# Segment 0 of the gated recurrence placed inside the last six groups of the projection, its loads reordered, GpSimd's first key copies tied to the last masks

## The chip, the cores and the metric

The kernel runs on one core of one Trainium2 chip, in one launch. The metric is the time of one execution on the device, in microseconds (us), as the median of several runs. A core has five engines that work side by side, each through its own instruction stream: TensorE (PE in the profile; PEld is its weight load), VectorE (DVE), ScalarE (ACT), GpSimd (POOL) and SyncE (SP, which here only issues DMAs). They order each other by semaphores. SBUF is the memory that the engines work on, PSUM the banks into which TensorE writes.

## The reference: what is computed

One layer of a hybrid decoder: an input projection, two token mixers on its result, gates, an output projection and a layer norm. There are 2048 prompt tokens and 64 sample tokens. Mixer A is a dilated sliding-window attention. The part around the change is mixer B, a gated linear recurrence with 4 heads and a state of 128 x 128 per head:

```
h = x @ w_in                      # split into qa, ka, va, ga, qb, fb, ib, gb
f = lb + (1 - lb) * sigmoid(fb);  k = 1 - f;  v = ib;  q = silu(qb) * 128 ** -0.5
S_t = diag(f_t) S_{t-1} + k_t v_t^T;   o_t = S_t^T q_t        # per head
a_out = attention(qa, ka, va) * silu(ga);  b_out = rmsnorm(o) * silu(gb)
y = layernorm(2 ** 0.25 * x + concat(a_out, b_out) @ w_out)
```

## The kernel before

The program is written by hand as one instruction stream for each engine, in five stages: a projection with the features on partitions (`project_transposed`: q, k and the forget gate), a second projection with the tokens on partitions (`project_natural`: v, i and the two gates), the prompt's recurrence (`hgrn_prompt`), the prompt's attention and the output projection (`attend_and_project`). The streams of the last four are concatenated, engine by engine, in `build`: each engine ends one stage and goes into the next by itself, held only by semaphores.

**The second projection** is 68 groups (`NGR`), numbered `n`. A group is 8 k steps of 3 matmuls (the exact product of split fp32 values: high x high, high x low, low x high), L757, with 512 columns each, into one of two PSUM banks. Two groups make one tile `j` of 128 tokens; the last tile, groups 66 and 67, has the 64 sample tokens. VectorE splits the x of a tile (`split_x`, L487 and L489), ScalarE evacuates each group (`evacuate`, L668), SyncE stores it to `projN` (L381). Between the groups, by a schedule in `n`, the samples' recurrence and attention are done; the last of these steps, the values of the eighth sample batch (L824), is behind group 60 (`LAST + 4`). Once SyncE has loaded the masks and q and the sigmoid of the gate for segments 0 and 1 (behind group 57, `load_segment`, L870 and L871), ScalarE makes the keys `kd` and forget factors `fd` of segment 0 beside groups 61 to 64, one head each (L740, L742).

**The recurrence** cuts the prompt into 4 segments of 512 tokens (`NSEG`, index `s`), and each into 4 chunks of 128. A segment has 18 scores (`NA`, index `j`): 4 of diagonal blocks (`ND`, L1121) and 14 for 7 levels of halves, two head pairs each (L1131). A diagonal score is 4 matmuls in fp32, a level's 8; the profile shows each such matmul as two. A level's score reads `qd` and `kd`; VectorE then widens both by the forget factors (`widen`: three tensor_tensor, L1058, L1059, L1061), which the score two places later waits for, and copies the score out of PSUM under a mask (`keep`: L1071 for diagonal blocks, L1080 for levels). Three PSUM banks hold scores. Before the first level VectorE forms `qd` by `first_products` (L1051). The state work of a segment stands between the scores of the next: `turn_keys` (L1143) behind scores 0 to 3, then, by the tuples `DELTA` and `OUT`, `delta` (L1154) and `read_out` (L1165, L1166) behind scores 4 to 11 in turns. ScalarE copies the turned keys (L1008) and the outputs (L1013), and takes their squares (L995); VectorE updates the state (`advance`, L1089). So segment 0 has only scores on TensorE, as nothing precedes it. Its diagonal scores start behind group 67, and TensorE takes 18 of them in a row.

**Loads and buffers.** Buffers of the recurrence come in pairs, `s % 2`. SyncE's `load(s)` waits until segment `s - 2` is done with q and gates, loads them and the values `v` (L948, from `projN`). In the loop, `load(s + 1)` stands behind `store(s - 1)`, which waits for ScalarE's copy of the last output of that segment. ScalarE's `decays(s)` (L984, L987) makes keys and forget factors of segment 1 ahead of all outputs and of segment 2 and 3 behind the outputs of segments 0 and 1. The buffers lie where the projection's were, so that what overlies its x, weights or stage waits for `group_done` or `stage_free`.

**GpSimd** clears `at0` behind the last samples and `at1` behind the last group, loads the first pair of heads' keys and queries (L878), and sorts them by dilation: `sort(0, 1)` and `sort(0, 2)`, three copies of 128 x 2048 each (L1420). The first waits for segment 3's fourth score (`a_done`), the second stands behind a pair load that waits for the squares of segment 3. Attention (scores L1783, minima L1529, exponentials L1686, turns L1797, values L1811) needs the first sorted keys at its ninth unit; its first three units are scored between the last read-outs.

## Time and profile before

| | before |
|---|---|
| median of 3 runs | 1592.74 us (1588.07 to 1593.78) |
| the profiled execution, its time | 1590.03 us |
| its span, first to last instruction | 1588.2 us |
| TensorE busy | 1530.3 us (96%) |
| VectorE busy | 774.5 us (49%) |
| ScalarE busy | 502.5 us (32%) |
| GpSimd busy | 442.4 us (28%) |
| mean granted TensorE clock | 0.966 |

Times in the profile are microseconds from the start of the span. The granted clock is a share of TensorE's full 2.4 GHz; the shares between come from stretches at 2.4 and at 1.2 GHz. A matmul's duration overlaps the next one's, so the cost of a matmul is read from start to start.

### The profile page before, as it was taken

Reading aid. Unit: us, or ns where it says so; the run is one execution under the profiler, and the core shown is the slowest. Engines: PE = TensorE matmul, PEld = TensorE weight load, DVE = VectorE, ACT = ScalarE, POOL = GpSimd, SP = SyncE. Lnnn points to the kernel's source line nnn. Section 1 sums busy time; section 2 is a strip of 40 time slices with the busy share of each in tenths; the row PEclk is TensorE's granted clock in tenths of the full one; section 3 lists DMA queues with packets and bytes.
Section 4 is the critical chain, followed back from the end, with each engine's and each line's share of the span. In section 5 each row is a group of like instructions: output and inputs, shape, how many; then the busy total and the mean of one; then the engine's idle time right before and its main releaser. Section 6 shows DMA issues by size and latency. Waiting matters only on the chain.

```text
span 1588.2 us, 25524 instructions
## 1 busy us (share of the span) xinstructions
PE 1530.3 (96%) x9802; PEld 1374.1 (87%) x9802; DVE 774.5 (49%) x1941; ACT 502.5 (32%) x1426; POOL 442.4 (28%) x281
## 2 busy tenths in 40 slices
PE   7999999998999999899999999889999999999997
PEld 7999999996788777677788999789999999888885
DVE  6022010004323214121215799867677777798884
ACT  5111111113110114122322032228677777432231
POOL 1233210000420000000001000306987779344442
PEclk9999999998999999999998699799999999999998
DMA  9999996234695867866665558749896981976641
GB/s 309 339 329 352 340 322 187 81 111 131 205 296 178 316 213 256 305 213 212 200 204 129 125 186 234 215 150 241 170 207 149 203 184 63 292 240 199 220 159 53
DMA packets 174501, 338.34 MB, mean 213 GB/s; under 512 B 15635, under 2 KB 115283, under 8 KB 165523
## 3 DMA queue, kind: packets, MB, share of 16 engines
q1 hardware_dynamic: 141452, 169.18, 35.1%
q10 hardware_dynamic: 22432, 111.29, 21.9%
q0 software_dynamic: 10512, 56.48, 13.1%
q8 instruction: 65, 1.06, 0.3%
q14 instruction: 40, 0.33, 0.1%
HBM read 262.25 MB, written 155.39 MB: 263 GB/s over the span
## 4 chain that ended last, share of the span: by engine, by line
PE 66%; DMA 4%; DVE 4%; ACT 1%; issue 1%; SPq 0%; DVEq 0%; ACTq 0%
PE banks L757 21%; PE banks L1846 11%; PE banks L1811 7%; PE banks L1131 7%; PE banks L1783 6%; PE banks L1797 4%; DMA spare<-in_xT 2%; DMA partials<-a_stage 2%; PE banks L824 1%; PE banks L1121 1%; PE banks L806 1%; PE banks L1154 1%; PE banks L1165 1%; PE banks L1166 1%; PE banks L1827 1%
## 5 line engine op out<-in xcount | busy, mean ns | idle before, releaser
L256 PE MATMUL acc<-xhi,whi 128*128 128x424 f32 (+1 forms) x640 | 227.3, 355 | 8.2 <-DVE xlo L235 8.2
L757 PE MATMUL banks<-nwhi,nxhi 128*128 128x512 f32 (+1 forms) x544 | 219.3, 403 | 11.8 <-DVE nwlo L494 6.6
L256 PE MATMUL acc<-xlo,whi 128*128 128x424 f32 (+1 forms) x640 | 227.0, 355 | 0.0
L256 PE MATMUL acc<-xhi,wlo 128*128 128x424 f32 (+1 forms) x640 | 226.9, 355 | 0.0
L1420 POOL CAST a_sorted<-a_plain 128x2048 fp32r<-128x2048 f32 x45 | 172.2, 3882 | 178.7 <-PE banks L1121 144.6
L757 PE MATMUL banks<-nwlo,nxhi 128*128 128x512 f32 (+1 forms) x544 | 214.4, 394 | 0.0
L757 PE MATMUL banks<-nwhi,nxlo 128*128 128x512 f32 (+1 forms) x544 | 214.1, 394 | 0.0
L1686 ACT ACTIVATE a_prob<-a_prob,a_stage 128x256 f32<-128x256 f32 (+1 forms) x384 | 174.1, 454 | 76.1 <-DVE a_stage L1529 73.7
L1529 DVE CUSTOM_DVE_ANT_0 a_prob<-banks,a_bias 128x256 f32<-128x256 f32 (+1 forms) x384 | 125.3, 364 | 77.6 <-PE banks L1783 69.1
L1811 PE MATMUL banks<-a_v,a_probT 128*128 128x64 f32 x1200 | 157.6, 269 | 2.9 <-DVE a_probT L1541 2.8
L1811 PEld LDWEIGHTS banks<-a_v,a_probT 128*128 128x128 f32 x1200 | 150.1, 193 | 4.3 <-DVE a_probT L1541 3.4
L487 DVE CAST nxhi<-spare 128x1024 fp32r<-128x1024 f32 (+1 forms) x34 | 24.9, 732 | 251.2 <-DMA spare<-in_xT 175.8
L225 DVE CAST whi<-wraw 128x1024 fp32r<-128x1024 f32 x16 | 14.9, 932 | 258.8 <-PE acc L256 166.5
L668 ACT ACTIVATE nstage<-banks 128x512 f32<-128x512 f32 (+1 forms) x68 | 40.6, 597 | 312.8 <-PE banks L757 312.6
L757 PEld LDWEIGHTS banks<-nwhi,nxhi 128*128 128x128 f32 (+1 forms) x544 | 101.5, 187 | 41.4 <-DVE nxlo L489 11.6
L275 ACT ACTIVATE stage<-acc 128x424 f32<-128x424 f32 (+1 forms) x80 | 41.7, 524 | 296.4 <-PE acc L256 295.9
L1131 PE MATMUL banks<-qd,kf 128*128 128x64 f32 x896 | 126.8, 307 | 8.4 <-DVE kf L1061 7.9
L1131 PEld LDWEIGHTS banks<-qd,kf 128*128 128x128 f32 x896 | 124.5, 225 | 9.9 <-issue 9.8
L256 PEld LDWEIGHTS acc<-xhi,whi 128*128 128x128 f32 x640 | 121.1, 189 | 10.6 <-issue 8.5
L256 PEld LDWEIGHTS acc<-xhi,wlo 128*128 128x128 f32 x640 | 121.1, 189 | 2.1
L256 PEld LDWEIGHTS acc<-xlo,whi 128*128 128x128 f32 x640 | 121.1, 189 | 2.1
L757 PEld LDWEIGHTS banks<-nwhi,nxlo 128*128 128x128 f32 (+1 forms) x544 | 101.4, 186 | 24.6 <-issue 1.4
(214 smaller groups left out, 2552.4 us busy)
## 6 DMA issues: line engine op xcount, KB each, us to landing
a_plain<-split_qk POOLq DMA_DIRECT2D x48, 512.0 KB, 12.9
out_kwin_s<-in_cache_kT ACTq DMA_DIRECT2D x8, 2048.0 KB, 19.9
split_qk<-spare POOLq DMA_DIRECT2D x16, 1024.0 KB, 14.5
spare<-in_xT SPq DMA_DIRECT2D x32, 512.0 KB, 7.1
projN<-nstage SPq DMA_DIRECT2D x32, 512.0 KB, 6.2
qg<-in_cache_kT ACTq DMA_DIRECT2D x8, 2048.0 KB, 11.3
kf<-in_cache_v ACTq DMA_DIRECT2D x8, 2048.0 KB
out_kwin_s<-in_cache_kT ACTq DMA_DIRECT2D x8, 2032.0 KB, 29.6
```

The costliest lines, as they stand in the source:

```text
L256: mm = pe.matmul(acc[:, j, 0:n], w[:, u, k], x[:, k, c0:c0 + n], start=(k == 0 and a == 0), stop=(k == KD - 1 and a == 2))
L275: nc.scalar.activation(stage[:, u, c0:c0 + n], acc[:, j, 0:n], func).then_inc(bank_free, 1)
L668: nc.scalar.activation(stage[0:m, u, g * H:(g + 1) * H], acc[0:m, n % 2], ACT.Copy if j < NTL else ACT.Silu).then_inc(evacuated, 1)
L757: mm = pe.matmul(acc[0:m, n % 2], x[:, u, k, 0:m], w[:, k, g * H:(g + 1) * H], start=(k == 0 and b == 0), stop=(k == KD - 1 and b == 2))
L1131: mm = pe.matmul(a_ps[:, i % 3, a * CH // 2:(a + 1) * CH // 2].rearrange("p (n j) -> p n j", j=w), kd[u][:, h, t0:t0 + CH], late, start=Tr ...
L1420: nc.gpsimd.tensor_copy(dst[:, n].rearrange("p (r m) -> p r m", r=d), src[:, n].bitcast(F32).rearrange("p (m r) -> p r m", r=d)).then_inc( ...
L1529: ins = nc.vector.tensor_tensor_reduce(prob[:, n % 4, w, 2 * P - m:], s_ps[:, n % 3, w * 2 * P + 2 * P - m:(w + 1) * 2 * P], bias[g % 2][: ...
L1686: ins = nc.scalar.activation(pr, pr, ACT.Exp, bias=to[:, DA + 1:DA + 2], scale=-1.0, accum_out=to[:, DA:DA + 1])
L1783: mm = pe.matmul(s_ps[:, n % 3, w * 2 * P + (2 - m) * P:(w + 1) * 2 * P], source[:, 0, q0:q0 + P], source[:, 1 + a, k0:k0 + m * P], start= ...
L1797: mm = pe.transpose(t_ps[:, n % 3, a * P:(a + 1) * P], prob[:, n % 4, w, place * P:(place + 1) * P], ident[:])
L1811: mm = pe.matmul(o_ps[:, (n // 4) % 2, col:col + DA], probT[:, n % 3, a], v[g % 2][:, c, vt, x * DA:(x + 1) * DA], start=(a == 0 or ts[a - ...
L1846: mm = pe.matmul(z_ps[w][0:n, g], m[:, w, k, 0:n], ww[:, g * H:(g + 1) * H], start=(k == 0 and a == 0), stop=(k == KD - 1 and a == 2))
```

## The change

- TensorE issues the 18 scores of segment 0 inside groups 62 to 67, ahead of the k steps numbered in `SLOTS` (k step 0 is the first of group 62): diagonal blocks ahead of steps 6, 7, 8 and 9, levels ahead of 11, 13, 16, 18, 21, 24, 26, 29, 31, 34, 37, 39, 42 and 44. The function `score` is moved out of `tensor` for this and otherwise unchanged. The recurrence's own stream starts with segment 1.
- ScalarE makes the keys of segment 0 behind group 60's evacuation and its forget factors behind group 61's; those of segment 1, one head each, behind groups 63 to 66.
- VectorE's last x split (tile 33) goes behind the ninth score of segment 0. The first memset of the state moves from segment 0 to segment 1.
- `kf1`, `qd1`, `at0` and `qd0` now lie where no buffer lives that groups 62 to 67 use.
- SyncE loads v of segment 0 behind the last group, then q and gates of segment 2 at once; in the loop, q and gates of segment `s + 2` are loaded behind the values of `s + 1`.
- `DELTA` and `OUT` go back by two scores.
- GpSimd's `sort(0, 1)` waits for all masks of segment 3.

```diff
@@ -330,7 +330,7 @@
             sem(f"d_{n}") for n in ("v_landed", "const", "bias_landed", "zeroed", "q_done", "qk_done", "min_done", "nm_done"))
         e_done, r_done, t_done, pt_done, pv_done, o_done = (
             sem(f"d_{n}") for n in ("e_done", "r_done", "t_done", "pt_done", "pv_done", "o_done"))
-        first["samples_done"], first["bias_spread"] = o_done, b_repeated
+        first["samples_done"], first["bias_spread"], first["out_free"] = o_done, b_repeated, out_free
...
+            first["last_split"] = lambda: split_x(NTL * NPASS - 1)
...
-                if n % 2 and j + 2 < NTL * NPASS:
+                if n % 2 and j + 2 < NTL * NPASS - 1:
                     split_x(j + 2)
...
@@ -731,16 +732,15 @@
                 if n == 2 * NTL - 1:
                     for k in range(KD):
                         round_w(3, k)
-                if LAST + EACH <= n < LAST + EACH + HB:
-                    h, (kd0, fd0) = n - LAST - EACH, (first["kf"][:, 0], first["kf"][:, 1])
-                    if h == 0:
-                        act.wait_ge(first["qk_landed"][0], 32)
-                        act.wait_ge(pv_done, NB)
-                    lb, oml, noml = (lbs_[:, m, h:h + 1] for m in (1, 2, 3))
-                    nc.scalar.activation(kd0[:, h], first["sg"][:, 0, h], ACT.Identity, bias=oml, scale=noml
-                                         ).then_inc(first["kd_done"], 1)
-                    nc.scalar.activation(fd0[:, h], first["sg"][:, 0, h], ACT.Identity, bias=lb, scale=oml
-                                         ).then_inc(first["fk_done"], 1)
+                if n == LAST + EACH - 1:
+                    act.wait_ge(pv_done, NB)
+                    first["keys"](act, 0, range(HB))
+                if n == LAST + EACH:
+                    first["forgets"](act, 0, range(HB))
+                if NGR - 5 <= n < NGR - 1:
+                    h = n - NGR + 5
+                    first["keys"](act, 1, range(h, h + 1))
+                    first["forgets"](act, 1, range(h, h + 1))
...
+                    if n >= NGR - 6:
+                        first["early_scores"](pe, KD * (n - NGR + 6) + k)
...
+        kf1, qd1, at0, qd0 = sb("kf1", [P, 2, HB, SEG]), wide("qd1"), attn("at0"), wide("qd0")
+        khn0, ost0, v31, ost1 = (rows(n) for n in ("khn0", "ost0", "v31", "ost1"))
+        v30, at1, khn1 = rows("v30"), attn("at1"), rows("khn1")
+        S = sb("S", [P, 2, HB, DB])
+        qd, at, khn, v, ost = (qd0, qd1), (at0, at1), (khn0, khn1), (v30, v31), (ost0, ost1)
+        kd, fd = ([first["kf"][:, m], kf1[:, m]] for m in range(2))
...
-        TURN, DELTA, OUT = (0, 1, 2, 3), (4, 6, 8, 10), (5, 7, 9, 11)
+        TURN, DELTA, OUT = (0, 1, 2, 3), (6, 8, 10, 12), (7, 9, 11, 13)
+        SLOTS = [6 + j for j in range(ND)] + [11 + 13 * j // 5 for j in range(NA - ND)]
...
-            def load(s):
+            def load_rows(s):
                 u, t0 = s % 2, s * SEG
                 if s >= 2:
-                    sp.wait_ge(fk_done, HB * (s - 1))
-                    sp.wait_ge(q1_done, NG2 * (s - 1))
-                    sp.wait_ge(a_done, NA * (s - 2) + ND)
-                    load_segment(sp, projT, s, q, sg, qk_landed)
-                    for m in range(2):
-                        sp.wait_ge(first["stage_free"][m], 16 * (T // P + 1))
                     sp.wait_ge(o_done, NCK * (s - 1))
                 sp.dma_start(v[u][:], projN[t0:t0 + SEG, WB:2 * WB].rearrange("(c p) v -> p c v", p=P)
                              ).then_inc(v_landed[u], 16)
+
+            def reload_segment(s):
+                sp.wait_ge(fk_done, HB * (s - 1))
+                sp.wait_ge(q1_done, NG2 * (s - 1))
+                sp.wait_ge(a_done, NA * (s - 2) + ND)
+                load_segment(sp, projT, s, q, sg, qk_landed)
 
...
-            load(0)
             sp.wait_ge(first["group_done"], NGR)
+            load_rows(0)
+            reload_segment(2)
             for u in range(2):
                 sp.wait_ge(first["stage_free"][u], 16 * (T // P + 1))
-            load(1)
+            load_rows(1)
...
-                    load(s + 1)
+                    load_rows(s + 1)
+                if s >= 1 and s + 2 < NSEG:
+                    reload_segment(s + 2)
...
+        def keys(act, s, heads):
+            u = s % 2
+            act.wait_ge(qk_landed[u], 32 * (s // 2 + 1))
+            for h in heads:
+                nc.scalar.activation(kd[u][:, h], sg[:, u, h], ACT.Identity, bias=oml[:, h:h + 1], scale=noml[:, h:h + 1]
+                                     ).then_inc(kd_done, 1)
+
+        def forgets(act, s, heads):
+            u = s % 2
+            for h in heads:
+                nc.scalar.activation(fd[u][:, h], sg[:, u, h], ACT.Identity, bias=lb[:, h:h + 1], scale=oml[:, h:h + 1]
+                                     ).then_inc(fk_done, 1)
+
+        first["keys"], first["forgets"] = keys, forgets
+
         def scalar(act):
             def decays(s):
                 u = s % 2
-                act.wait_ge(qk_landed[u], 32 * (s // 2 + 1))
-                if s >= 2:
-                    act.wait_ge(s_done, NCK * (s - 1) + 1)
-                    act.wait_ge(t_done, NCK * (s - 1))
-                for h in range(HB):
-                    ins = nc.scalar.activation(kd[u][:, h], sg[:, u, h], ACT.Identity, bias=oml[:, h:h + 1], scale=noml[:, h:h + 1])
-                ins.then_inc(kd_done, HB)
-                for h in range(HB):
-                    ins = nc.scalar.activation(fd[u][:, h], sg[:, u, h], ACT.Identity, bias=lb[:, h:h + 1], scale=oml[:, h:h + 1])
-                ins.then_inc(fk_done, HB)
+                act.wait_ge(s_done, NCK * (s - 1) + 1)
+                act.wait_ge(t_done, NCK * (s - 1))
+                keys(act, s, range(HB))
+                forgets(act, s, range(HB))
 
...
+                if s == 1:
+                    for x in range(2):
+                        act.wait_ge(first["stage_free"][x], 16 * (T // P + 1))
...
-            decays(1)
-            for u in range(2):
-                act.wait_ge(first["stage_free"][u], 16 * (T // P + 1))
...
                 first_products(s)
-                if s == 0:
+                if s == 1:
                     dve.wait_ge(first["group_done"], NGR)
                     nc.vector.memset(S[:, 0], 0.0).then_inc(s_done, 1)
...
+                    if s == 0 and j == 2 * ND:
+                        first["last_split"]()
...
+        def early_scores(pe, slot):
+            if slot == SLOTS[0]:
+                pe.wait_ge(const, 16 * 3)
+                pe.wait_ge(qk_landed[0], 32)
+                pe.wait_ge(kd_done, HB)
+            if slot in SLOTS:
+                score(pe, 0, SLOTS.index(slot))
+
+        first["early_scores"] = early_scores
...
-            pe.wait_ge(const, 16 * 3)
-            for s in range(NSEG):
+            for s in range(1, NSEG):
                 pe.wait_ge(qk_landed[s % 2], 32 * (s // 2 + 1))
                 pe.wait_ge(kd_done, HB * (s + 1))
                 for j in range(NA):
-                    score(s, j)
-                    if s >= 1:
-                        if j in TURN:
-                            turn_keys(s - 1, TURN.index(j))
-                        if j in DELTA:
-                            delta(s - 1, DELTA.index(j))
-                        if j in OUT:
-                            read_out(s - 1, OUT.index(j))
+                    score(pe, s, j)
+                    if j in TURN:
+                        turn_keys(s - 1, TURN.index(j))
+                    if j in DELTA:
+                        delta(s - 1, DELTA.index(j))
+                    if j in OUT:
+                        read_out(s - 1, OUT.index(j))
...
+            sp.wait_ge(keep["ms_done"], NCK * (NSEG - 1))
...
-            pool.wait_ge(keep["a_done"], 18 * (NSEG - 1) + 4)
-            pool.wait_ge(keep["q1_done"], HB // 2 * NSEG)
+            pool.wait_ge(keep["mask_done"], 18 * NSEG)
             sort(0, 1)
```

## Rows read from the trace of the kernel before

**Rows 1.** Page, the chain that ended last, share of the span by engine
```profile
PE 66%; DMA 4%; DVE 4%; ACT 1%; issue 1%; SPq 0%; DVEq 0%; ACTq 0%
```

**Rows 2.** Busy time by stretch: us, busy (count) of each engine, clock, DMA share, GB/s
```profile
862.90:900.40 37.50, 37.49 (x176) 37.50 (x177) 26.44 (x45) 0.00 (x0) 0.00 (x0) 0.50 0.85 200
932.60:944.20 11.60, 11.41 (x98) 10.98 (x96) 11.24 (x24) 1.93 (x10) 0.00 (x0) 1.00 0.87 298
1014.90:1026.80 11.90, 11.88 (x57) 11.90 (x58) 11.79 (x21) 0.00 (x0) 0.00 (x0) 0.51 0.56 172
```

**Rows 3.** Timeline of TensorE, segment 0: start, us, engine, line, what, [idle before]
```profile
852.19 3.73 PE L1121 MATMUL banks<-qg,kf 128*128 128x128 f32 x32
862.91 37.78 PE L1131 MATMUL banks<-qd,kf 128*128 128x64 f32 x176 [1.08 <-DVE kf L1061]
900.49 1.81 PE L1121 MATMUL banks<-qg,kf 128*128 128x128 f32 x7
```

**Rows 4.** Timeline of VectorE, from segment 1 to the start of segment 2
```profile
909.51 0.69 DVE L1058 TENSOR_TENSOR qd<-qd,kf 128x512 f32<-128x512 f32 x1 [1.23 <-PE banks L1131]
946.11 0.72 DVE L1080 COPY_PREDICATED at<-lmask,banks 128x512 f32<-128x512 int32 x1
949.99 2.36 DVE L1051 TENSOR_TENSOR qd<-qg,kf 128x1024 f32<-128x1024 f32 x2 [3.16 <-issue]
956.41 0.69 DVE L1058 TENSOR_TENSOR qd<-qd,kf 128x512 f32<-128x512 f32 x1 [0.55 <-PE banks L1131]
```

**Rows 5.** Timeline of ScalarE, the keys of segment 2
```profile
944.15 0.81 ACT L984 ACTIVATE kf<-qg,bounds 128x512 f32<-128x512 f32 x1 [9.45 <-DMA qg<-projT]
```

**Rows 6.** Timeline of VectorE, segment 3
```profile
1004.07 2.23 DVE L1058 TENSOR_TENSOR qd<-qd,kf 128x512 f32<-128x512 f32 x1 [1.50 <-PE banks L1131]
1010.60 4.17 DVE L1061 TENSOR_TENSOR kf<-kf 128x512 f32<-128x512 f32 x1
1052.81 0.73 DVE L1080 COPY_PREDICATED at<-lmask,banks 128x512 f32<-128x512 int32 x1
```

**Rows 7.** Timeline of GpSimd, the first and the second set of copies
```profile
1001.85 12.37 POOL L1420 CAST a_sorted<-a_plain 128x2048 fp32r<-128x2048 f32 x3 [144.57 <-PE banks L1121]
1084.82 11.24 POOL L1420 CAST a_sorted<-a_plain 128x2048 fp32r<-128x2048 f32 x3
```

**Rows 8.** Timeline of TensorE, scores, a turn and a read-out at full clock
```profile
904.76 1.06 PE L1121 MATMUL banks<-qg,kf 128*128 128x128 f32 x8
905.70 0.63 PE L1143 MATMUL banks<-ident,kf 128*128 128x128 f32 x4
910.25 1.90 PE L1131 MATMUL banks<-qd,kf 128*128 128x64 f32 x16
911.99 0.44 PE L1165 MATMUL banks<-S,qd 128*128 128x128 f32 x2
```

**Rows 9.** Timeline of TensorE, projection matmuls directly after the samples' attention values
```profile
779.82 0.50 PE L757 MATMUL banks<-nwhi,nxhi 128*128 128x512 f32 x1
780.16 0.39 PE L757 MATMUL banks<-nwlo,nxhi 128*128 128x512 f32 x1
780.39 0.40 PE L757 MATMUL banks<-nwhi,nxlo 128*128 128x512 f32 x1
```

**Rows 10.** Timeline of SyncE's queue, the loads of v for segments 0 and 1
```profile
853.69 2.85 SPq L948 DMA_DIRECT2D v<-projN  x2
```

**Rows 11.** Tile v, time to landing: the load for segment 0, then for segment 1
```profile
DMA to landing us min/median/max: 9.8/9.8/9.8
DMA to landing us min/median/max: 24.2/24.2/24.2
```

**Rows 12.** Timeline of TensorE, the first scores that read sorted keys
```profile
1082.76 0.71 PE L1783 MATMUL banks<-a_sorted 128*128 128x128 f32 x4
```

**Rows 13.** VectorE by line and shape, 1085 to 1096 us, then 1073 to 1084 us
```profile
L1529 DVE CUSTOM_DVE_ANT_0 a_prob<-banks,a_bias 128x256 f32<-128x256 f32 x11 | 4.3, 421 | 1.5 <-PE banks L1783 1.5
L1529 DVE CUSTOM_DVE_ANT_0 a_prob<-banks,a_bias 128x256 f32<-128x256 f32 x11 | 4.3, 422 | 6.8 <-PE banks L1783 6.8
```

55 lines of the change are left out of this document (28 added, 27 removed).

## The prediction, made before the changed kernel was run

> **What bounds the kernel now.** I read the chain of waits of the page first: TensorE makes 66% of it, no other engine more than 4% [rows 1]. So an edit pays by the time that it takes out of TensorE's own sequence, and other engines' work counts where TensorE waits for it or runs slowly. The busy shares hide the second kind, so I listed the granted clock by stretch around the change. From 862.9 to 900.4 us TensorE is shown 100% busy at 0.50 of its clock, that is 1.2 of 2.4 GHz, and from 1014.9 to 1026.8 at 0.51; in between, from 932.6, it is 1.00 [rows 2]. Then I read the timelines of each engine there. They show four places that the change touches. (a) Segment 0 of the recurrence: only scores, from 852.19 to 900.49 us, with no state work to put between them; TensorE and VectorE hand each other work, and after a gap of 1.08 us the clock is at half [rows 3]. (b) Segments 1 to 3: from its first widening at 909.51 to its last mask's end at 946.83 VectorE hardly rests, so there it sets the pace and not TensorE. (c) The starts of segments 2 and 3: VectorE idles over 3 us [rows 4], as TensorE does, behind ScalarE's keys, and ScalarE waited 9.45 us for the loads [rows 5], which SyncE issued behind the store of the segment before. (d) Segment 3: GpSimd's three copies run from 1001.85 to 1014.2 us [rows 7], and three tensor_tensor of VectorE in a row, otherwise 0.69 us each, are stretched: the first takes 2.23, the last 4.17 us [rows 4, 6]. TensorE has to wait for them and then runs at half clock [rows 2].
>
> **Step A, segment 0 between the groups.** The 48.30 us from 852.19 to 900.49 leave the sequence [rows 3]. The same 18 scores come back inside groups 62 to 67. At full clock a score of diagonal blocks takes 0.94 us (904.76 to 905.70) and one of a level 1.74 us (910.25 to 911.99) [rows 8], so 4 x 0.94 + 14 x 1.74 = 28.1 us. No row shows a switch in the middle of an accumulation; the nearest is the samples' attention between groups: the first matmul behind it is followed after 0.34 us, the next after the usual 0.23 us [rows 9]. I take 0.1 us into a score and 0.1 out of it, 18 x 0.2 = 3.6 us, with 0 and 0.5 us as ends (0 to 9 us); below 0 is excluded, as the scores' matmuls and loads remain what they are. Is the pace kept? A k step is three matmuls or 0.68 us and the slots of the levels lie two or three steps apart, so such a score comes every 2 x 0.68 + 1.74 + 0.2 = 3.3 us or more. VectorE takes 37.3 us in segment 1 for 14 levels and four updates, under 2.7 us a level [rows 4]. So no stall. The six groups are 144 matmuls of 0.227 us, 32.7 us, so group 62 starts at 819.5 and the first score is due six k steps later, at 823.6. Its keys, four activations of 0.8 us [rows 5], move up from groups 61 to 64 into group 60; the forget factors follow group 61, done by 823, VectorE's products (2.4 us, as in segment 1) by 826.5, and the first level's score comes at 831. The last x split (1.1 us) now stands behind the ninth score, some 10 us before group 66 needs it. ScalarE's eight activations of segment 1 (6 us, formerly behind the groups) go between evacuations over 5 us apart: hidden. Net of A: 48.3 - 28.1 - 3.6 = 16.6 us gained.
>
> **Step A2, the start of segment 1.** Now 9.02 us pass from its first score to the first widening (900.49 to 909.51) [rows 3, 4], the first part at half clock. Coming from the groups the clock is full: four scores with a turn each, the turn half as many rows as the score, are 4 x (0.94 + 0.47), and the fifth score is 1.74 [rows 8], together 7.4 us. VectorE is ready earlier: its last mask of segment 0 ends about when the groups do; then 2.4 us of products, 0.5 of memset, 3.3 of masks. Gain 1.6 us. GpSimd's memset, still tied to the last group, is done before the first mask. New on this path: segment 0's values are wanted by the first delta, now behind the seventh score, 7.4 + 1.74 + 1.74 + 0.4 of waiting = 11.3 us after the last group. They can only be loaded when the groups are done. Now they are issued 1.5 us after that [rows 10] and land in 9.8 us, together 11.3 [rows 11]: no stall to speak of. The other load of this size took 24.2 us, which is the bad end (14.4 us).
>
> **Step B, loads ahead of stores.** Segment 2's q and gates are asked for directly after the last group and segment 3's one segment early, so ScalarE finds them. Its keys must still follow the squares of the last read-out, which moves two scores back, to some 27.4 us after the first widening; with 2 us of copy and squares the keys are done at 32.4 and the forget factors at 35.3 us, where TensorE's last score ends at 34 and VectorE's last mask at 37.3 us. Both are in time, the second by 2 us. What is late next is VectorE: 2.4 us of products, 3.2 of masks, and about 0.9 us of waiting for the fifth score, 6.5 us. A segment then lasts 37.3 + 6.5 = 43.8 us from widening to widening, where it is 46.9 (909.51 to 956.41) and 47.7 us (956.41 to 1004.07) [rows 4, 6]. Gain 3.1 + 3.9 = 7.0 us. The shift of DELTA and OUT changes no amount of VectorE's work: nothing.
>
> **Step C, GpSimd's copies.** Segment 3 lasts 49.5 us from its first widening to its last mask's end (1004.07 to 1053.54) [rows 6], against 37.3 us in segment 1. The copies move behind the last mask: 12.2 us gained. They take 12.4 us there and are first read at 1082.76 us, 29 us after that mask [rows 12]. The second set starts at 1084.82 [rows 7] behind a pair load that waits for the squares of segment 3: unchanged. Under the copies now lie four state updates of VectorE and the first attention minima, whose first input is in PSUM. Such minima take a mean of 421 ns beside the second set of copies and 422 before it [rows 13], so they aren't held; no row shows a state update beside a copy. I take nothing, as for the minima, and 8 us as the other end (two updates held 3.5 us each, as the last tensor_tensor is, and a little clock); below nothing is excluded, since nothing runs faster for the copies. The Trainium skill, "SBUF — State Buffer", section "Who interferes with whom", says that a VectorE instruction with two SBUF inputs contends with a GpSimd one that reads SBUF and one with a single SBUF input doesn't. The stretched tensor_tensor and the minima agree with it; by it the updates cost nothing, by the bound 8 us.
>
> **Sum.** 16.6 + 1.6 + 7.0 + 12.2 = 37.4 us. The profiled execution took 1590.03 us (span 1588.2), so 1590.0 - 37.4 = 1552.6; it lies 2.7 us under the median of the three runs, 1592.74, so 1555.3, given as 1555. Attention behind it only shifts.
>
> **Rivals.**
> 1. The copies hold the tail. The updates stand between TensorE's last read-outs, so they would be on the path: 8 us, 1563. For it: the stretched instructions [rows 6]. Against: those read SBUF twice, and the minima aren't stretched [rows 13]. 12%.
> 2. Segment 0's values land late, as the second such load did: 14.4 us, 1570. For it: GpSimd's pair load and SyncE's other loads run in the same 30 us, and 2 MB are added [rows 11]. Against: the values are first in their queue. 8%.
> 3. The loads are there, but segments 2 and 3 start no earlier, because ScalarE's keys, now behind a later read-out, become the wait: none of the 7.0 us, 1562. The margin of 2 us speaks against it. 7%.
> 4. Slower than before: the clock falls to half inside the groups. The place is the work from group 62 to 67 (32.7 + 28.1 + 3.6 = 64.4); each us of that work at half clock costs one us more, so it would have to last over 37 us of that work to eat the gain, and over the whole stretch it would give 1555 + 64.4 = 1619. For it: the same scores ran 37.5 us at 0.50 with TensorE fully busy and did not get the clock back by themselves [rows 2, 3]. Against: from 932.6 to 944.2, a stretch of nearly nothing but such scores, it kept 1.00 [rows 2], and here each is followed by six or more projection matmuls, and there is no gap. 4%. The Trainium skill, "TensorE: Matmul & The Clock Gate", "What's actually happening", has sustained activity release the throttle; by that rule the clock would soon come back and this rival be void. The trace doesn't bear it out: the stretch at 0.50 is fully busy.
>
> **How the numbers follow.** Forecast 1555 with 66% (own range 1549 to 1562: switches 0 to 9 us, spread of the runs), the rivals 12, 8, 7 and 4%, the rest 3% for what I don't see. The low end is the forecast less the 3.6 us of switches and 3.4 of spread, 1548. The high end takes in rivals 1 to 3, 1572. About 0.5% (8 us) is what a measurement of this kernel can tell from no change. Faster 94%, same 2%, slower 4%.
>
> **What would show it.** A: the six groups with 18 scores last 64 to 65 us at a clock near 1.0, and segment 1's first score follows the last group directly; VectorE's masks of segment 0 lie among the groups. A2: no wait for v at the first delta. B: no DMA wait ahead of the keys of segments 2 and 3, widening to widening 43.8 us. C: no VectorE tensor_tensor above 1 us in segment 3, 37.3 us from widening to mask; the four updates at 1.1 us each. Wrong it would be if a switch costs over 1 us, if a segment stays at 47 us, or if a new gap of TensorE shows up in the first 15 us of segment 1 or of attention.

## The result and the profile after

The changed kernel takes 1558.26 us in the median (1554.11 to 1562.63, 4 runs); the kernel before, run on the same chip, 1593.26 us (1588.07 to 1596.22, 4 runs). The ratio is 0.9784 (95% interval 0.9769 to 0.9798), so 35.0 us faster, where 1555 us and a gain of 37.4 were predicted.

| | after |
|---|---|
| median of 4 runs | 1558.26 us |
| the profiled execution, its time | 1562.63 us |
| its span | 1560.8 us |
| TensorE busy | 1506.6 us (97%) |
| VectorE, ScalarE, GpSimd busy | 768.2, 502.0, 440.1 us |
| mean granted TensorE clock | 0.984 |

The page of after, its chain that ended last, share of the span by engine: TensorE still sets the time [rows 1].

```profile
PE 63%; DVE 4%; DMA 4%; ACT 2%; issue 1%; POOL 1%; SPq 0%; DVEq 0%; ACTq 0%; POOLq 0%
```

This execution was the longest of the four. Its group 62 starts at 823.43 us, 4.0 us later than in the trace of before (819.39), although the code ahead of it is the same, and it loses some 4 us more far behind the change, in attention. So I compare from the start of group 62 to the first score on sorted keys: 263.4 us before (819.39 to 1082.76), 227.3 after (823.43 to 1050.69), 36.1 us less. Fifteen us on, 1.0 of these is given back (below). The 35.1 us left agree with the medians. By the steps of the prediction:

| stretch | before | after | gain | predicted |
|---|---|---|---|---|
| A: groups 62 to 67 and the 18 scores of segment 0 | 81.1 | 61.45 | 19.65 | 16.6 |
| A2: first score of segment 1 to first widening | 9.02 | 7.48 | 1.5 | 1.6 |
| B: first widening of segment 1 to that of segment 3 | 94.6 | 92.0 | 2.5 | 7.0 |
| C: first widening of segment 3 to its last mask | 49.5 | 38.5 | 11.0 | 12.2 |
| last mask to first sorted score | 29.2 | 27.8 | 1.4 | 0 |

Timeline of TensorE in after: the first score inside group 62, with the k step behind it, and a level's score inside group 67; then segment 1's first score and its turn; last, the start of segment 3.

```profile
827.51 1.05 PE L1144 MATMUL banks<-qg,kf 128*128 128x128 f32 x8
828.32 0.48 PE L759 MATMUL banks<-nwhi,nxhi 128*128 128x512 f32 x1
828.64 0.40 PE L759 MATMUL banks<-nwlo,nxhi 128*128 128x512 f32 x1
...
829.11 1.05 PE L1144 MATMUL banks<-qg,kf 128*128 128x128 f32 x8
...
880.39 1.89 PE L1154 MATMUL banks<-qd,kf 128*128 128x64 f32 x16
882.09 0.42 PE L759 MATMUL banks<-nwhi,nxhi 128*64 128x512 f32 x1
...
884.88 1.05 PE L1144 MATMUL banks<-qg,kf 128*128 128x128 f32 x8
885.77 0.60 PE L1177 MATMUL banks<-ident,kf 128*128 128x128 f32 x4
...
975.14 1.44 PE L1144 MATMUL banks<-qg,kf 128*128 128x128 f32 x8 [2.06 <-issue]
```

Read the starts: a diagonal score holds the sequence for 0.81 us (827.51 to 828.32), a level's for 1.70 (880.39 to 882.09), and the k step behind a diagonal score takes 0.79 us instead of 0.68 (828.32 to 829.11), as its second matmul starts 0.32 us after its first and not 0.23. Nothing idles. Segment 3, however, starts after a gap of 2.06 us.

Busy time by stretch in after, columns as in [rows 2]: groups 62 to 67, segment 1, 25 us across the start of segment 2, segment 3, and the 15 us ahead of the first sorted score.

```profile
823.50:884.90 61.40, 61.40 (x402) 53.01 (x401) 42.84 (x67) 12.02 (x18) 0.00 (x0) 1.00 0.13 40
892.40:930.90 38.50, 36.38 (x318) 35.63 (x318) 36.90 (x73) 13.15 (x44) 0.00 (x0) 1.00 1.12 289
916.20:941.20 25.00, 23.42 (x203) 22.66 (x202) 22.42 (x41) 10.25 (x24) 0.00 (x0) 1.00 1.00 307
984.40:1022.90 38.50, 35.46 (x310) 34.77 (x310) 36.85 (x72) 7.51 (x36) 0.00 (x0) 1.00 0.67 195
1035.80:1050.60 14.80, 11.72 (x92) 11.53 (x91) 9.34 (x41) 13.11 (x60) 0.00 (x0) 0.88 0.62 198
```

Both stretches at half clock in [rows 2] have gone. The DMA engines, nearly idle beside the groups (0.13), are saturated in segment 1 and beyond.

VectorE in after: the first wait inside segment 1, the products and the first widening of segment 3, and the first of the four last updates.

```profile
922.62 0.69 DVE L1080 TENSOR_TENSOR qd<-qd,kf 128x512 f32<-128x512 f32 x1 [1.00 <-PE banks L1154]
977.95 2.36 DVE L1073 TENSOR_TENSOR qd<-qg,kf 128x1024 f32<-128x1024 f32 x2 [2.30 <-issue]
984.38 0.69 DVE L1080 TENSOR_TENSOR qd<-qd,kf 128x512 f32<-128x512 f32 x1 [0.90 <-PE banks L1154]
1026.45 1.12 DVE L1111 SCALAR_TENSOR_TENSOR S<-S,kf,banks 128x128 f32<-128x128 f32 x4 [3.60 <-PE banks L1188]
```

Three of these updates (1026.45, 1029.57 and 1032.70 us) lie beside GpSimd's copies, which end at 1034.5; the fourth (1035.85) and the first minima (from 1036.89) come behind them. No stretched tensor_tensor is left, where [rows 6] has 2.23 and 4.17 us. GpSimd in after, both sets of copies, and TensorE's first score on the second set:

```profile
1022.91 11.62 POOL L1453 CAST a_sorted<-a_plain 128x2048 fp32r<-128x2048 f32 x3 [132.94 <-DVE at L1102]
1054.06 11.21 POOL L1453 CAST a_sorted<-a_plain 128x2048 fp32r<-128x2048 f32 x3
```
```profile
1065.32 0.66 PE L1815 MATMUL banks<-a_sorted 128*128 128x128 f32 x4 [0.43 <-POOL a_sorted L1453]
```

The second set is now a wait: TensorE idles 0.43 us for it. From the first sorted score to this one TensorE takes 14.63 us, where it took 13.63 before, so from there on the lead over the kernel before is 1.0 us smaller: 0.6 us of that stands at this score, the other 0.4 ahead of the second sorted score.

Last, ScalarE and SyncE's queue in after. ScalarE had finished the squares at 967.6 us and then waited 4.51 us for segment 3's gates, where [rows 5] has 9.45; the second row is the first of four copies of the samples' cache, 2 MB each, that ScalarE issues beside segment 2's keys.

```profile
972.11 0.81 ACT L990 ACTIVATE kf<-qg,bounds 128x512 f32<-128x512 f32 x1 [4.51 <-DMA qg<-projT]
```
```profile
922.23 0.57 ACTq L130 DMA_DIRECT2D out_vwin_s<-in_cache_v  x1
```

SyncE's queue (start, how long the issue held the queue, line, what):

```profile
889.41 19.11 SPq L971 DMA_DIRECT2D a_ident<-in_ident  x1
...
916.16 25.00 SPq L896 DMA_DIRECT2D a_v<-projN  x4
941.21 10.29 SPq L898 DMA_DIRECT2D a_v<-projN  x1
951.55 6.30 SPq L961 DMA_DIRECT2D o_b<-ost  x1
957.89 0.91 SPq L949 DMA_DIRECT2D v<-projN  x1
958.91 2.22 SPq L872 DMA_DIRECT2D qg<-projT  x1
```

The loads that attention needs much later (`a_ident`, `a_v`) hold the queue from 889 to 951 us, and the store of segment 0 to 958. Segment 3's gates are asked for at 958.91, though everything they wait for in the code was long done.

### The profile page after: what moved, and what is told of

Same layout as the page of the kernel before. It is cut to its first block, busy times and chain, and to the rows that moved or that the text cites. A ratio compares the mean times of both kernels' runs of the same rounds, so it can differ in the third digit from the quotient of the medians.

```text
span 1560.8 us, 25524 instructions
## 1 busy us (share of the span) xinstructions
PE 1506.6 (97%) x9802; PEld 1348.0 (86%) x9802; DVE 768.2 (49%) x1941; ACT 502.0 (32%) x1426; POOL 440.1 (28%) x281
## 4 chain that ended last, share of the span: by engine, by line
PE 63%; DVE 4%; DMA 4%; ACT 2%; issue 1%; POOL 1%; SPq 0%; DVEq 0%; ACTq 0%; POOLq 0%
PE banks L759 22%; PE banks L1878 11%; PE banks L1843 7%; PE banks L1815 5%; PE banks L1154 4%; PE banks L1829 4%; DMA spare<-in_xT 2%; PE banks L826 1%; DMA partials<-a_stage 1%; DVE at L1102 1%; PE banks L808 1%; PE banks L1859 1%; PE banks L1144 1%; DVE kf L1081 1%; PE banks L1199 1%
## 5 line engine op out<-in xcount | busy, mean ns | idle before, releaser
L759 PE MATMUL banks<-nwhi,nxhi 128*128 128x512 f32 (+1 forms) x544 | 220.6, 405 | 13.3 <-DVE nwlo L494 6.9
L256 PEld LDWEIGHTS acc<-xhi,whi 128*128 128x128 f32 x640 | 121.4, 190 | 11.7 <-issue 7.9
L759 PEld LDWEIGHTS banks<-nwlo,nxhi 128*128 128x128 f32 (+1 forms) x544 | 101.8, 187 | 21.4 <-issue 1.2
L1154 PEld LDWEIGHTS banks<-qd,kf 128*128 128x128 f32 x896 | 105.0, 192 | 6.4 <-issue 4.8
## 6 DMA issues: line engine op xcount, KB each, us to landing
qg<-in_cache_kT ACTq DMA_DIRECT2D x8, 2048.0 KB, 11.6
```

The lines of the kernel that those rows point to most:

```text
L256: mm = pe.matmul(acc[:, j, 0:n], w[:, u, k], x[:, k, c0:c0 + n], start=(k == 0 and a == 0), stop=(k == KD - 1 and a == 2))
L759: mm = pe.matmul(acc[0:m, n % 2], x[:, u, k, 0:m], w[:, k, g * H:(g + 1) * H], start=(k == 0 and b == 0), stop=(k == KD - 1 and b == 2))
L1154: mm = pe.matmul(a_ps[:, i % 3, a * CH // 2:(a + 1) * CH // 2].rearrange("p (n j) -> p n j", j=w), kd[u][:, h, t0:t0 + CH], late, start=Tr ...
```

## The experiments

Each time is a median, set against runs of the kernel before on the same chip (their medians lie between 1592.6 and 1593.4 us). Segment lengths are from the first widening to the end of the last mask, read from the trace of each kernel. Of the versions of the changed kernel, only e3_old_loads and e9_sort_twice have an interval clear of its own (ratio 0.9769 to 0.9798). For the others the traces decide. In the order of the sections below the versions are e1_copies_late, e2_copies_in_seg3, e9_sort_twice, e3_old_loads, e10_loads_first, e7_attention_loads_later, e5_old_turns, e6_old_turns_2_3 and e8_both, and e4_fill_seg0; I call them e1 to e10 for short.

### GpSimd's copies alone

```diff
-            pool.wait_ge(keep["a_done"], 18 * (NSEG - 1) + 4)
-            pool.wait_ge(keep["q1_done"], HB // 2 * NSEG)
+            pool.wait_ge(keep["mask_done"], 18 * NSEG)
```

> The kernel before with one edit: GpSimd's first three sort copies wait for all masks of segment 3. Theory (the copies hold VectorE's tensor_tensor, and only those): segment 3 from first widening to last mask goes from 49.5 to 37.3 us, the tail stays, total 11 to 12 us less. Rival (the copies hold the state updates too): 3 to 8 us less, with updates over 1.1 us in the tail.

1581.78 us, ratio 0.9913 (0.9879 to 0.9947), so 11.6 us faster. Segment 3 takes 37.31 us (1003.79 to 1041.10) instead of 49.47, the three updates beside the copies 1.12 us each, as the fourth behind them. Step C is worth what the working said, 12.2 us in the trace.

### Extra copies in segment 3 of the changed kernel

```diff
+            pool.wait_ge(keep["a_done"], 18 * (NSEG - 1) + 4)
+            pool.wait_ge(keep["q1_done"], HB // 2 * NSEG)
+            pool.wait_ge(pair_landed[0], 96)
+            for n in range(3):
+                nc.gpsimd.tensor_copy(plain[0][:, n], plain[0][:, n].bitcast(F32)).then_inc(keep["extra"], 1)
+            pool.wait_ge(keep["extra"], 3)
             pool.wait_ge(keep["mask_done"], 18 * NSEG)
```

> The changed kernel plus three extra GpSimd copies of the same size (in place, same values) at the place where the kernel before had them, behind the fourth score of segment 3; all else as in the changed kernel. Theory: 11 to 12 us more, three tensor_tensor of 2 to 4.3 us and a TensorE gap of 6 us with half clock behind it. Rival (copies beside segment 3 are harmless once the other waits are gone): under 3 us more.

1562.69 us, ratio 0.9803 (0.9778 to 0.9828), 4.4 us over the changed kernel. The expectation missed, for a reason that the trace gives: these copies, in place and without a stride, took 6.03 us together and not 12. GpSimd, then VectorE in segment 3:

```profile
977.14 6.03 POOL L1502 CAST a_plain<-a_plain 128x2048 fp32r<-128x2048 f32 x3 [89.80 <-PE banks L1144]
```
```profile
979.28 2.13 DVE L1080 TENSOR_TENSOR qd<-qd,kf 128x512 f32<-128x512 f32 x1 [0.89 <-PE banks L1154]
981.34 2.37 DVE L1081 TENSOR_TENSOR kf<-kf 128x512 f32<-128x512 f32 x1
983.74 0.69 DVE L1083 TENSOR_TENSOR kf<-kf 128x512 f32<-128x512 f32 x1
```

Two tensor_tensor are held and the third, behind the last copy, is not. Segment 3 takes 46.15 us (38.47 without), 7.7 more; in this run its loads were in time, which gave some 2.4 back. The size was left in doubt, so I ran the real copies twice.

### The strided copies made twice

The same edit, with the three copies of `sort(0, 1)` in the place of the plain ones:

```diff
+                nc.gpsimd.tensor_copy(sorted_[0][:, n].rearrange("p (r m) -> p r m", r=DILS[1]),
+                                      plain[0][:, n].bitcast(F32).rearrange("p (m r) -> p r m", r=DILS[1])).then_inc(keep["extra"], 1)
```

> The changed kernel, with the same three strided copies of GpSimd also made once more where they stood before, at segment 3's fourth score (the set behind the last mask stays as it is). Theory (a tensor_tensor of VectorE is held to the end of the copy that it meets, so the price follows the copies' length): the set takes 11 to 12 us as at its old place, where three unstrided copies took 6.0 us and cost segment 3 7.7 us; segment 3 goes from 38.5 to 48.5 to 50 us from widening to last mask, and the time is 1558 + 11 = 1569 us. Rival (the price is a fixed stall at the start of a set, whatever the length): segment 3 again 46 us and 1563 to 1566 us.

1564.97 us, ratio 0.9833 (0.9815 to 0.9851), 6.7 us over the changed kernel. GpSimd and VectorE:

```profile
977.23 12.29 POOL L1502 CAST a_sorted<-a_plain 128x2048 fp32r<-128x2048 f32 x3 [90.23 <-PE banks L1144]
```
```profile
979.37 2.28 DVE L1080 TENSOR_TENSOR qd<-qd,kf 128x512 f32<-128x512 f32 x1 [0.89 <-PE banks L1154]
981.58 4.29 DVE L1081 TENSOR_TENSOR kf<-kf 128x512 f32<-128x512 f32 x1
985.90 4.18 DVE L1083 TENSOR_TENSOR kf<-kf 128x512 f32<-128x512 f32 x1
```

Segment 3 takes 49.37 us, as before the change (49.47): 10.9 us for 12.3 of copies, 7.7 for 6.0. The rival, a price that doesn't depend on the length, is out. But the price is not in proportion to the length either. VectorE's three instructions are stretched by 3.1 us in the run before this one and by 8.7 us here, and that part follows the copies. The rest, 4.6 and 2.2 us, lies behind: TensorE idled 3.55 and 9.10 us for VectorE and then ran at a clock of 0.50 until about 996 us in both traces. The time, 1565, lies under the 1569 expected; segment 3 starts 2.0 us earlier in this run than in the trace of after, since its loads were in time, and the rest is within the intervals.

### The loads behind the store again

```diff
             load_rows(0)
-            reload_segment(2)
...
                 if s >= 1 and s + 1 < NSEG:
+                    reload_segment(s + 1)
                     load_rows(s + 1)
-                if s >= 1 and s + 2 < NSEG:
-                    reload_segment(s + 2)
```

> The changed kernel with the q and gate loads of segments 2 and 3 back behind the store of the segment before. Theory: the starts of segments 2 and 3 wait for loads again, widening to widening 47 to 49 us for segment 1 (44.8 in the changed kernel) and about 48 for segment 2 (47.2, as segment 3's load is late there anyway), total 3 to 5 us more. Rival (VectorE bounds, loads hidden): within 1 us.

1571.52 us, ratio 0.9861 (0.9835 to 0.9886), 13.3 us over the changed kernel: far more than either theory gave. TensorE at the starts of segments 2 and 3:

```profile
934.70 2.05 PE L1142 MATMUL banks<-qg,kf 128*128 128x128 f32 x8 [10.29 <-issue]
972.54 7.59 PE L1152 MATMUL banks<-qd,kf 128*128 128x64 f32 x64
987.24 2.05 PE L1142 MATMUL banks<-qg,kf 128*128 128x128 f32 x8 [7.11 <-issue]
```

The gaps were about 3 us in the kernel before, whose scores behind the last read-out of segment 1 are these:

```profile
932.59 11.69 PE L1131 MATMUL banks<-qd,kf 128*128 128x64 f32 x96
```

Two things add up, and I had named neither. First, this kernel keeps the shift of `DELTA` and `OUT`. The store, and the loads behind it, wait for the last read-out, and behind that lie 7.6 us of scores (972.54 to 980.1) where there were 11.7. That is 4.1 us more of waiting, which alone gives the gap ahead of segment 3: its loads take as long as before (11.5 us from the copy of the last output to the keys, 11.4 before). Second, at segment 2 that path takes 14.7 us: its gates go out at 919.64 us, beside the attention loads, and ScalarE waits 12.75 us for them. So the early loads are a condition of the shift, and not only a gain of 7 us beside it. What the old loads cost without the shift was not run.

### The early loads alone, in the kernel before

```diff
             sp.wait_ge(first["group_done"], NGR)
+            reload_segment(2)
...
                     load(s + 1)
+                if s >= 1 and s + 2 < NSEG:
+                    reload_segment(s + 2)
```

Here `load(s)` no longer loads q and gates.

> The kernel before with step B alone: q and gates of segment 2 are asked for behind the last group, those of segment 3 in the loop one segment early, behind the values of segment 2. Theory of the prediction: both starts are 6.5 us long, the segments 43.8 us, gain 7.0 us, 1586 us. Rival, from the changed kernel's trace: segment 3's loads stand in SyncE's queue behind the loads for attention and land late, so only segment 2 gains: 3 us, 1590 us.

1584.51 us, ratio 0.9949 (0.9932 to 0.9965), 8.1 us faster. The first widenings stand at 911.03, 954.70 and 998.36 us, so 43.67 and 43.66 us from one to the next; the working said 43.8. Taken alone, step B was right. In SyncE's queue the last attention load went out at 891.95 us, with all of segment 1 still ahead, and segment 3's gates at 935.97:

```profile
882.42 9.48 SPq L894 DMA_DIRECT2D a_v<-projN  x4
891.95 0.83 SPq L896 DMA_DIRECT2D a_v<-projN  x1
935.41 0.44 SPq L944 DMA_DIRECT2D v<-projN  x1
935.97 1.05 SPq L870 DMA_DIRECT2D qg<-projT  x1
```

### The attention loads behind segment 3's

In the changed kernel, `load_bias` and `load_values(0)` move into SyncE's loop, to its third pass, behind segment 3's q, gates and values:

```diff
             sp.wait_ge(first["bias_spread"], 32)
-            load_bias(sp, rep_p, keep["bias"][0], 0, keep["bias_landed"][0])
-            load_values(sp, projN, keep["v"][0], 0, keep["v_landed"][0])
...
+                if s == 2:
+                    load_bias(sp, rep_p, keep["bias"][0], 0, keep["bias_landed"][0])
+                    load_values(sp, projN, keep["v"][0], 0, keep["v_landed"][0])
```

> The changed kernel with SyncE's bias and value loads for attention moved from ahead of the segment loop to behind the loads of segment 3. Theory (the late start of segment 3 comes from these loads holding SyncE's queue, so that the store of segment 0 and the loads behind it are issued some 25 us late): segment 3's loads are issued before 935 us, ScalarE does not wait for them, TensorE's gap of 2 us ahead of segment 3 is gone, widening to widening 44.8 us in place of 47.2, total 2 us less. Rival (the values for attention then land late): a new wait at the first values matmul of attention, total 3 us or more above the changed kernel.

1555.48 us (1552.86 to 1556.64), ratio 0.9762 (0.9749 to 0.9775), 2.8 us under the changed kernel. SyncE's queue and ScalarE's keys of segment 3:

```profile
917.82 0.37 SPq L961 DMA_DIRECT2D o_b<-ost  x1
...
918.84 1.05 SPq L872 DMA_DIRECT2D qg<-projT  x1
```
```profile
963.75 0.81 ACT L991 ACTIVATE kf<-qg,bounds 128x512 f32<-128x512 f32 x1
```

The wait of 4.51 us and TensorE's gap of 2.06 us are gone, segment 3's start is 6.3 us long as segment 2's, and `a_v`, asked for at 966 us, is still in time. The time agrees; its interval overlaps that of the changed kernel, so the verdict rests on the trace.

How much the late loads cost differs from one execution to the next. e2_copies_in_seg3 and e9_sort_twice have the same code for SyncE as the changed kernel, and it takes 44.8 and 45.2 us in them from segment 2's first widening to segment 3's, against 47.2 in the trace of after. ScalarE waits 1.02 and 2.54 us for the gates. ScalarE's first cache copy and SyncE's queue in e2_copies_in_seg3:

```profile
919.59 0.57 ACTq L130 DMA_DIRECT2D out_vwin_s<-in_cache_v  x1
```
```profile
911.07 9.62 SPq L896 DMA_DIRECT2D a_v<-projN  x4
...
921.53 30.19 SPq L961 DMA_DIRECT2D o_b<-ost  x1
...
952.99 1.21 SPq L872 DMA_DIRECT2D qg<-projT  x1
```

Here the attention loads are out by 921.5 us, and it is the store of segment 0 that is held for 30 us. In all five traces that have the attention loads ahead of the loop and the early loads (after, e2, e5, e6, e9) the cache copies are issued at 918 to 922 us, and segment 3's gates only at 952 to 959, whatever stood in the queue meanwhile. In this kernel the store, the values and the gates of segment 3 go out from 917.8 to 921.1 us, around the cache copies at 918.5, and each took 1.2 us or less; the four `a_v` loads that follow the next cache copies (963.3) were held 37.6 us. So what the attention loads do is to push these loads behind the cache copies. A kernel with the cache copies moved would test it and was not run.

### The state work at its old places

```diff
-        TURN, DELTA, OUT = (0, 1, 2, 3), (6, 8, 10, 12), (7, 9, 11, 13)
+        TURN, DELTA, OUT = (0, 1, 2, 3), (4, 6, 8, 10), (5, 7, 9, 11)
```

> The changed kernel with the state work back behind scores 4 to 11 in all segments. The changed kernel's VectorE waits 1.0 us for a score in each of segments 1 to 3 and takes 38.5 us from first widening to last mask, where the kernel before took 37.3. Theory (the two-score shift costs that): 37.3 us again in segments 2 and 3, but in segment 1 the first delta now comes 3.5 us ahead of the landing of segment 0's values, so nothing is won there; total 2 us less. Rival (the shift is neutral and the 1.2 us come from elsewhere): segments stay at 38.5 us, total 1 to 3 us more through the wait for the values.

1560.12 us, ratio 0.9797 (0.9781 to 0.9813), 1.9 us over the changed kernel; 2 under it was expected. Segments 2 and 3 did get shorter, 37.35 and 37.33 us instead of 38.48. But segment 1 takes 42.57. TensorE there:

```profile
890.93 1.60 PE L1188 MATMUL banks<-v,khn 128*128 128x128 f32 x8 [1.79 <-DMA v<-projN]
892.33 3.51 PE L1154 MATMUL banks<-qd,kf 128*128 128x64 f32 x16
```

The first delta now comes before segment 0's values: a wait of 1.79 us, and behind it a score takes 3.51 us instead of 1.90. From 892 to 899 us the granted clock was 0.55. So the shift pays in segment 1, 4.1 us (42.57 for 38.49), and costs 1.1 us in each of the others. Step A2 had used this without saying so: its first delta stands "behind the seventh score", which is the shift's doing. From the first widening of segment 2 to that of segment 3 this kernel takes 43.67 us, Step B's 43.8.

### The shift in segment 1 only, without and with the later attention loads

```diff
+                    back = 0 if s == 1 else 2
-                    if j in DELTA:
-                        delta(s - 1, DELTA.index(j))
+                    if j + back in DELTA:
+                        delta(s - 1, DELTA.index(j + back))
```

and the same for `read_out` and for VectorE's `advance`.

> The changed kernel with the state work back behind scores 4 to 11 in segments 2 and 3 only; segment 1 keeps the shift. Theory: 37.3 us in segments 2 and 3, 38.5 in segment 1, no wait for values, total 2 to 3 us less than the changed kernel. Rival: no change within 1 us.

1556.18 us (1555.32 to 1559.2), ratio 0.9773 (0.9759 to 0.9787), 2.1 us under the changed kernel, as expected. The segments take 38.49, 37.33 and 37.33 us. The start of segment 3 is still late (9.8 us), as ScalarE waits 9.22 us for its gates.

> Both edits of the two runs before in one kernel. Theory: segments 1 to 3 at 38.5, 37.3 and 37.3 us, both boundaries at 6.4 us, total 4 to 5 us less than the changed kernel, about 1553 where that one is 1558. Rival: the two do not add up, 1556 or more.

1553.91 us (1552.22 to 1559.42), ratio 0.9761 (0.9744 to 0.9779), 4.4 us under the changed kernel and 39 under the one before: the fastest version. Its segments take 38.49, 37.36 and 37.34 us and both starts 6.3. From each other the three variants are not separated by their times, only by these lengths.

### Filling TensorE in segment 0 of the kernel before

```diff
                 for j in range(NA):
                     score(s, j)
+                    if s == 0 and j >= ND:
+                        pe.matmul(s_ps[:, 0], ident[:], q[:, 0, 0], start=True, stop=True)
```

> The kernel before with one extra fp32 matmul of 512 columns, whose result nobody reads, behind each of the 14 level scores of segment 0, some 0.9 us each at full clock. Theory (segment 0's slowness is mostly the clock, which falls because the scores alone do not keep it up): the clock stays at or returns to 1.0, segment 0 takes about 42 us in place of 48.3, total 6 us less although work is added. Rival (the clock stays at half): 14 x 1.7 = 24 us more. Third (the wait between TensorE and VectorE is what counts, clock or not): no change within 2 us.

1582.78 us, ratio 0.9929 (0.9904 to 0.9954): 10.6 us faster with 14 matmuls of 0.91 us more. Busy time by stretch, to be set beside the first row of [rows 2], and two scores with such a matmul between them:

```profile
862.00:899.80 37.80, 37.80 (x267) 31.38 (x265) 34.28 (x57) 1.79 (x3) 0.00 (x0) 1.00 0.92 208
```
```profile
858.52 1.07 PE L1176 MATMUL banks<-qg,ident 128*128 128x512 f32 x2
859.43 1.90 PE L1131 MATMUL banks<-qd,kf 128*128 128x64 f32 x16
861.17 1.07 PE L1176 MATMUL banks<-qg,ident 128*128 128x512 f32 x2
```

The clock is 1.00 where it was 0.50, there is no gap behind the first scores, TensorE is busy throughout, and segment 0 takes 40.67 us (853.22 to 893.89) instead of 48.30. So the scores' slowness came with the clock: had only the handing to and fro counted, the time would have stayed. The extra matmuls do two things at once, though: they put 512-column work between the scores, and they close the gaps of 0.42 and 1.08 us, behind the second of which the clock was at half. Which of the two keeps the clock up, this run doesn't say. Nor does it say how long the scores alone would take at full clock, as 28.1 + 14 x 0.91 = 40.8 us is TensorE's own work here; VectorE was busy for 35.3 us of it. The total fell by more than these 7.6 us because the start of segment 1 is shorter too (7.75 us from its first score to the first widening, for 9.02). With 0.8 us from segment 3's products on, the trace gives 9.65 us up to the first sorted score; the interval is 7.3 to 15.3 us.

## Why the prediction came out right, and where it did not

**Bound.** TensorE's sequence sets the time, and edits paid by what they took out of it.

**Step A, mis-sized by 3.1 us.** The failed term is the switch. Taking off the six groups' own 32.7 us, the 18 scores cost 28.75 us in all, 0.65 over the 28.1 that the rows of scores give: 0.04 us for a score with both its switches, where 0.2 was taken. The bound from below, 0, was the better one. The 0.1 us out of a score was right: the first matmul behind it is followed after 0.32 us (828.32 to 828.64), where [rows 9] has 0.34. The 0.1 us into it was wrong: an inserted diagonal score holds the sequence for 0.81 us and a level's for 1.70, less than the 0.94 and 1.74 of [rows 8], so "below 0 is excluded" did not hold for the way in. VectorE and the clock kept up, as argued. The scores now cost some 20 us less than the 48.3 us they had. At least 7.6 of these were half clock (e4_fill_seg0); how the rest divides between half clock and VectorE's pace was not separated.

**Step A2, right:** 7.48 us for 7.4. The values of segment 0 landed 9.2 us after 886.39, at 895.6, and the first delta stands at 896.34: a margin of 0.7 us.

**Step B, right alone and wrong beside A.** Alone it measures 43.7 us a segment and 8.1 us of time. In the changed kernel segments 1 and 2 last 44.8 and 47.2 us. Two things are missing from the working. First, SyncE's queue: I let segment 3's loads be asked for "one segment early" and did not count what stands ahead of them. In the changed kernel they come behind the attention loads in time, because step A takes away the 48 us in which these were served; and the cache copies that ScalarE issues beside segment 2's keys, at 944.17 us in the trace of before and at 922.23 now, fall on them as well. From 916.2 to 941.2 us the DMA engines are busy the whole time, at 307 GB/s. Moving the attention loads away removes the wait, which shows that they are what makes segment 3's loads late. That the queue is held by the cache copies behind which they push these loads is read from the times of seven traces (after, e2 and e5 to e9) and was not tried by itself. The wait cost TensorE 2.4 us in the trace of after, and 0 and 0.4 us in two others with the same code for SyncE. Second, the shift of `DELTA` and `OUT`.

**"The shift changes no amount of VectorE's work: nothing", wrong.** The amount is the same, but there is a wait: 1.1 us in each of segments 1 to 3. With the state work two places later, TensorE has a delta and a read-out between scores at a point where VectorE's levels have become short, and VectorE waits for a score: the 1.00 us at 922.62. Undone in segments 2 and 3, it gives 1.1 us each. In segment 1 the shift saves more than it costs, by letting segment 0's values land first, and it is also what makes late loads dear (e3_old_loads).

**Step C, right:** 12.2 us alone. In the changed kernel 11.0, the difference being the shift. The three updates beside the copies are not held; the bound of 8 us wasn't needed. In section "Who interferes with whom" of "SBUF — State Buffer" the Trainium skill says this of instructions with at most one SBUF input. The updates, scalar_tensor_tensor with one of their two tensor inputs in PSUM, took 1.12 us beside copies and 1.11 away from them, and tensor_tensor with both in SBUF up to 4.29 us: the traces agree. The prediction had put the fourth update and the first minima under the copies as well, and they come behind them.

**Tail.** Its 1.4 us are not the change's. From the last mask to the first sorted score e10_loads_first, with the copies at their old place, takes 27.85 us too, and e5_old_turns, with the copies at the new one, 29.1. The longer ones have a mean clock of 0.82 (before) and 0.85 (e5), the shorter 0.88 (after and e10) and 0.95 (e7, 27.87 us), so I put the difference down to the clock, which is read and not tried. The second set of copies as a new wait (1.0 us) was not foreseen. In the kernel before they ended 0.33 us ahead of the score that reads them. e1_copies_late and e10_loads_first, with one step each, wait for them as well (14.37 and 14.59 us from the first sorted score), so it isn't the sum of the steps that does it; what does is open.

**Rivals.** Copies holding the tail: no. Values of segment 0 late: not in the changed kernel; with the delta at its old place they are late by 1.79 us. Segments starting no earlier: for segment 3 in part, but by the loads and not by ScalarE's keys. Clock at half inside the groups: no, 1.00 throughout.

**Sum.** A 3.1 us better, B 4.5 worse (some 2.4 for the late loads and 2.2 for the shift), C 1.2 worse (the shift), the second copies 1.0 worse, the tail 1.4 better: 37.4 became 35.1. The total was nearer than its terms: errors of 3 to 4 us with opposite signs cancelled, which is luck.

## What to carry to other kernels

When a stretch of pure work is moved under another, ask what had been served in its time: here the attention loads had lived in segment 0's 48 us, and once it was gone they met the next segment's loads in the same queue, and pushed them behind the cache copies. A queue is costed by what stands ahead in it and how long each issue holds it, not by the time to land alone. An independent short group of matmuls can stand inside an accumulation at almost no price, and the matmuls around it cover the other engine's part. GpSimd's long copies were free where VectorE's instructions read PSUM and at most one tensor of SBUF.

## What the runs showed of the hardware that I had not expected

- TensorE was shown 100% busy for 37.5 us at a clock of 0.50 with nothing but scores [rows 2], and with 14 matmuls of 512 columns between the same scores, and no gap ahead of them, it never left 1.00 (e4_fill_seg0). Being busy did not bring the clock back by itself. The Trainium skill ("TensorE: Matmul & The Clock Gate", "What's actually happening") has sustained activity release the throttle; the stretch at 0.50, fully busy, doesn't agree with it.
- One issue can hold SyncE's queue for tens of us, and all that stands behind it waits. Busy DMA engines alone don't set how long: the four loads of `a_v` took 9.48 us to issue with the engines fully busy at 330 GB/s (e10_loads_first) and 25.00 at 307 GB/s (after), with the cache copies issued in between. A single one of them took 34.3 us right behind the cache copies (e7_attention_loads_later), and a plain store 30.2 (e2_copies_in_seg3).
- The copy of GpSimd that costs 3.9 us with a stride of the dilation took 2.0 us in place and without one (6.03 for three).
- A fp32 score can stand inside an open accumulation in another bank for 0.04 us beyond its own price, on average over 18: the step behind it is 0.1 us longer, and the score itself shorter than between turns and read-outs.
